# A decoder trunk on one core: the FFN's first product made token-stationary, its result turned by VectorE and moved by GpSimd's transfers

## The reference, cut to what matters

```
x = layer_norm(ALPHA * x + mixer(x) @ w_o)
up, gate = split(x @ w_in, 2)            # x 256 x 1024, w_in 1024 x 5632: up and gate 256 x 2816 each
up = causal_conv_over_tokens(up, width 3, one filter for each feature) + conv_b
f  = (gelu(up) * gate) @ w_out           # w_out 2816 x 1024
x = layer_norm(ALPHA * x + f)
```

## Time and profile before

| | |
|---|---|
| median of three runs | 600.32 us (600.27 to 600.74) |
| span of the profiled execution, first to last instruction | 598.3 us |
| TensorE matmuls busy | 589.4 us, 99%, 3216 instructions |
| VectorE busy | 464.9 us, 78% |
| ScalarE busy | 323.7 us, 54% |
| GpSimd busy | 50.5 us, 8% |
| read from HBM | 108.23 MB, 183 GB/s over the span |

### The profile page before, as it was taken

How to read it: one execution, slowest core, us unless ns; L and a number is a source line. 1 busy time by engine, 2 the same in 40 slices (tenths; PEclk the granted TensorE clock), 3 DMA queues, 4 the chain that set the end, 5 groups by cost and what they waited for, 6 DMA issues and landing times.

```text
span 598.3 us, 8585 instructions
## 1 busy us (share of the span) xinstructions
PE 589.4 (99%) x3216; PEld 501.1 (84%) x3216; DVE 464.9 (78%) x841; ACT 323.7 (54%) x520; POOL 50.5 (8%) x84
## 2 busy tenths in 40 slices
PE   8999999999999999999999999999999999999995
PEld 6887777898888888889888888889888888888894
DVE  4989994877777778777979797688677777777776
ACT  5756684265445444456445678935554555545430
POOL 6300000300000000000120003132000000000003
PEclk9999999999999999999999999999999999999998
DMA  8996865363556686554457955343755555755601
GB/s 306 296 341 215 261 186 189 139 223 109 184 191 209 211 280 211 192 169 173 172 203 222 302 177 186 108 140 101 251 191 182 188 170 204 242 172 201 210 2 70
DMA packets 82293, 116.38 MB, mean 195 GB/s; under 512 B 11292, under 2 KB 60236, under 8 KB 82252
## 3 DMA queue, kind: packets, MB, share of 16 engines
q1 hardware_dynamic: 80812, 111.64, 56.3%
q0 software_dynamic: 1152, 4.19, 2.1%
q10 hardware_dynamic: 288, 0.00, 0.0%
HBM read 108.23 MB, written 1.05 MB: 183 GB/s over the span
## 4 chain that ended last, share of the span: by engine, by line
PE 98%; DVE 1%; ACT 0%; DVEq 0%; issue 0%
PE wide L1294 18%; PE wide L1295 18%; PE wide L1296 18%; PE score L1501 11%; PE score L1507 6%; PE turn L1501 5%; PE outb L1501 5%; PE outb L1507 3%; PE turn L1507 3%; PE score L1307 1%; PE turn L1393 1%; PE outb L1419 1%; PE score L1296 1%; PE score L1295 1%; PE score L1294 1%; PE wide L1315 1%
## 5 line engine op out<-in xcount | busy, mean ns | idle before, releaser
L965 DVE TENSOR_TENSOR w_lo<-raw,w_hi 128x2048 fp32r<-128x2048 f32 (+1 forms) x120 | 211.0, 1776 | 60.6 <-ACT w_hi L772 60.4
L772 ACT ACTIVATE w_hi<-raw 128x2048 fp32r<-128x2048 f32 (+1 forms) x126 | 182.2, 1483 | 34.5 <-PE wide L1296 23.6
L1294 PE MATMUL wide<-w_hi,xT 128*128 128x512 f32 (+1 forms) x256 | 95.7, 374 | 0.3 <-DVE w_lo L1031 0.2
L1294 PE MATMUL wide<-w_hi,oT_hi 128*128 128x512 f32 x240 | 95.3, 397 | 0.0
L1295 PE MATMUL wide<-w_lo,oT_hi 128*128 128x512 f32 x240 | 93.7, 391 | 0.0
L1296 PE MATMUL wide<-w_hi,oT_lo 128*128 128x512 f32 x240 | 93.6, 390 | 0.0
L1296 PE MATMUL wide<-w_hi,xT 128*128 128x512 f32 (+1 forms) x256 | 93.0, 363 | 0.0
L1295 PE MATMUL wide<-w_lo,xT 128*128 128x512 f32 (+1 forms) x256 | 92.9, 363 | 0.0
L893 ACT ACTIVATE qT<-kT,conv_cols 128x256 f32<-128x256 f32 x36 | 21.7, 602 | 93.1 <-DVE kT L1198 93.1
L1501 PE MATMUL score<-xT,w_hi 128*128 128x512 f32 x288 | 68.3, 389 | 0.0
L1501 PEld LDWEIGHTS score<-xT,w_hi 128*128 128x128 f32 x288 | 53.9, 188 | 11.1
(11 more groups left out here) (182 smaller groups left out, 809.6 us busy)
## 6 DMA issues: line engine op xcount, KB each, us to landing
raw<-in_ffn_w_in SPq DMA_DIRECT2D x44, 1024.0 KB, 5.1
raw<-in_ffn_w_out SPq DMA_DIRECT2D x22, 1024.0 KB, 4.9
raw<-in_a_w_qkv SPq DMA_DIRECT2D x9, 1024.0 KB, 6.1
raw<-in_w_kv_shared SPq DMA_DIRECT2D x8, 1024.0 KB, 5.6
raw<-in_a_w_o SPq DMA_DIRECT2D x4, 1024.0 KB, 6.5
raw<-in_b_w_q SPq DMA_DIRECT2D x4, 1024.0 KB, 5.1
raw<-in_b_w_o SPq DMA_DIRECT2D x4, 1024.0 KB, 5.1
raw<-in_a_w_qkv SPq DMA_DIRECT2D x4, 512.0 KB, 7.7
```

The costliest lines, as they stand in the source:

```text
L772: ins = nc.scalar.activation(w_hi[c % RING][:, part], raw[c % RAW_RING][:, part], ACT.Copy)
L965: ins = nc.vector.tensor_tensor(w_lo[c % RING][:, part], raw[c % RAW_RING][:, part], w_hi[c % RING][:, part].bitcast(F32), ALU.subtract)
L1294: nc.tensor.matmul(dst, a_hi, b_hi, start=start, stop=False, skip_group_check=True)
```

## The change

- The first product of all groups is token-stationary. A chunk now holds four k-tiles of up and gate columns side by side (4 x 512 columns), loaded by two DMAs of 512 KB; a group is two such chunks. For each half of the tokens 8 products of 512 columns go to one bank: two banks a group, 48 matmuls. `features`, `last_features`, the first group's transposes on TensorE and VectorE's sums go.
- VectorE turns each bank in 32 x 32 blocks into `turned` (`turn_in`, two a group); GpSimd issues four DMAs of 32 partitions each (`in_move`) that make it feature-major in `in_moved`.
- ScalarE copies the up tiles out once more (`up`) beside the tap, and the gate is read from `in_moved`.
- The second product of a group comes behind the first product of the group two later; hidden tiles have a ring of 4 instead of 1 and 2. Behind the last first product stand now the whole second product of group 8, and then the quarters of groups 9 and 10 as before.
- The orders of ScalarE and VectorE are written anew, with the splits of a group's chunks ahead of its taps. Chunk numbers follow TensorE's new order. GpSimd loads the norm rows behind the sixth move.

```diff
+    def second_behind(i):
+        return [i - 2] if i >= 2 else []
@@ SP
+                def load_in(i):
+                    for h in range(2):
+                        load(ffn_chunk(layer, i, h),
+                             *[(lambda r, w=w: r.rearrange("p (k w n) -> p k w n", k=4, w=2)[:, :, w, :],
+                                w_in[:, 4 * h:4 * h + 4, w * DFF + i * 2 * P:w * DFF + (i + 1) * 2 * P]) for w in range(2)])
@@ GpSimd
+            def in_move(layer, i):
+                t = GROUPS * layer + i
+                pool.wait_ge(in_turned, ST * t + ST)
+                for a in range(4):
+                    pool.dma_start(in_moved[:, a, :], turned[32 * a:32 * a + 32, t % 2, :, :]).then_inc(in_carried, 16)
...
-                    pool.wait_ge(hidden_done, 2 * GROUPS * (n // 2) + GROUPS)
-                    load_norm(n)
+                    for i in range(GROUPS):
+                        in_move(n // 2, i)
+                        if i == GROUPS // 2:
+                            load_norm(n)
@@ ScalarE
+                def taps(i):
+                    t = GROUPS * layer + i
+                    act.wait_ge(in_carried, 64 * (t + 1))
                     for tt in range(2):
+                        if t > 0:
+                            act.wait_ge(conv_done, 2 * t + tt - 1)
+                        nc.scalar.activation(by_quarters(up[:, tt, :]), carried(tt), ACT.Copy)
+                        nc.scalar.activation(by_quarters(conv[:, tt, :]), carried(tt), ACT.Identity, ...).then_inc(tap_done, 1)
...
+                for i in range(GROUPS):
+                    split_hi(ffn_chunk(layer, i, 0) + RING)
+                    if i:
+                        make_h_hi(i - 1)
+                    if i < GROUPS - 1:
+                        split_hi(ffn_chunk(layer, i, 1) + RING)
+                        for n in second_behind(i):
+                            split_hi(ffn_chunk(layer, n, 2) + RING)
+                        taps(i)
+                        make_gelu(i)
+                    else:
+                        split_hi(ffn_chunk(layer, i, 1) + RING, 0)
+                        split_hi(ffn_chunk(layer, i, 1) + RING, 1)
+                        taps(i)
+                        make_gelu(i)
+                        make_h_hi(i)
+                        split_hi(ffn_chunk(layer, i - 2, 2) + RING, 0)
+                        split_hi(ffn_chunk(layer, i - 2, 2) + RING, 1)
@@ VectorE
+                def turn_in(i, st):
+                    t = GROUPS * layer + i
+                    dve.wait_ge(*((in_rows_done, t + 1) if st == 0 else (chunk_used, ffn_chunk(layer, i, 1) + 1)))
+                    if st == 0 and t >= 2:
+                        dve.wait_ge(in_carried, 64 * (t - 1))
+                    bank = (wide[0:2] if i == 0 else in_banks[(i - 1) % 2])[st]
+                    into = turned[:, t % 2, :, :].rearrange("p b (j s t) -> p b j s t", j=4, s=ST)
+                    nc.vector.transpose(into[:, :, :, st, :], bank[:, :].rearrange("p (j f b) -> p b j f", j=4, b=4)
+                                        ).then_inc(in_turned, 1)
...
+                for i in range(GROUPS):
+                    turn_in(i, 0)
+                    split_lo(ffn_chunk(layer, i, 0) + RING)
+                    turn_in(i, 1)
+                    if i:
+                        for tt in range(2):
+                            make_h_lo(i - 1, tt)
+                    if i < GROUPS - 1:
+                        split_lo(ffn_chunk(layer, i, 1) + RING)
+                        for n in second_behind(i):
+                            split_lo(ffn_chunk(layer, n, 2) + RING)
+                        add_taps(i)
+                        for tt in range(2):
+                            make_hidden(i, tt)
+                    else:
+                        split_lo(ffn_chunk(layer, i, 1) + RING, 0)
+                        split_lo(ffn_chunk(layer, i, 1) + RING, 1)
+                        add_taps(i)
+                        for tt in range(2):
+                            make_hidden(i, tt)
+                            make_h_lo(i, tt)
+                        if ffn_chunk(layer, i - 2, 2) + RING == SHARED:
+                            split_shared_lo()
@@ TensorE
+                def in_product(i):
+                    t = GROUPS * layer + i
+                    chunks = [ffn_chunk(layer, i, h) for h in range(2)]
+                    banks = wide[0:2] if i == 0 else in_banks[(i - 1) % 2]
+                    if i >= 3:
+                        pe.wait_ge(in_turned, ST * (t - 2) + ST)
+                    for h, st in ((0, 0), (1, 0), (0, 1), (1, 1)) if i == 0 else ((0, 0), (0, 1), (1, 0), (1, 1)):
+                        c = chunks[h]
+                        for k in range(4):
+                            kt = 4 * h + k
...
+                            if i == 0 and st == 0 and kt in (6, 7):
+                                x_transposes(2 * layer + 1, (kt - 4,))
...
+                            last = product(banks[st][:, :], xT_hi[:, kt, rs], xT_lo[:, kt, rs],
+                                           w_hi[c % RING][:, cols], w_lo[c % RING][:, cols], kt == 0, kt == KT - 1)
...
+                for i in range(GROUPS):
+                    in_product(i)
+                    for n in second_behind(i):
                         for st in range(ST):
                             for half in range(2):
+                                last = out_product(n, st, half)
                         last.then_inc(chunk_used, 1)
```

More of the change, by code:

```diff
@@ L349, in ffn_chunk, with raw_count @@
         if which == 2:
[L350 to L362, removed]
+            return base + (3 * i + 6 if i < GROUPS - 2 else 2 * GROUPS + i)
+        return base + (2 * i if i < 3 else 3 * i - 2) + which
+    def second_behind(i):
+        return [i - 2] if i >= 2 else []
+    IN_CHUNKS = {ffn_chunk(layer, i, h) for layer in range(LAYERS) for i in range(GROUPS) for h in range(2)}
+    def raw_count(c):
+        return sum(32 if n in IN_CHUNKS else 16 for n in range(c % RAW_RING, c + 1, RAW_RING))
     moves_ahead = {}
@@ L915, in ffn_group, with make_h_hi @@
-                    if peeled == "last":
-                        split_hi(cg + RING, 0)
-                        split_hi(cg + RING, 1)
-                    if peeled in ("second", "middle"):
-                        split_hi(cg + 1 + RING)
-                ffn_group(0, "first")
-                ffn_group(1, "second")
-                for i in range(2, GROUPS - 1):
-                    ffn_group(i, "middle")
-                ffn_group(GROUPS - 1, "last")
+                def make_h_hi(i):
+                    for tt in range(2):
+                        act.wait_ge(hidden_done, 2 * (GROUPS * layer + i) + tt + 1)
+                        if tt == 0 and i >= HIDDEN:
+                            act.wait_ge(chunk_used, ffn_chunk(layer, i - HIDDEN, 2) + 1)
+                        nc.scalar.activation(hT_hi[i % HIDDEN][:, tt, :], hidden[:, tt, :], ACT.Copy).then_inc(hhi_done, 1)
@@ L1529, in last_features @@
-                def last_features(banks, slot, free, free0, done0):
-                    for tt in range(2):
-                        pe.wait_ge(free, free0 + tt)
-                        for kt in range(KT):
-                            last = product(by_two(banks[tt])[:, 0, :], w_hi[slot][:, tile_cols(kt, tt)],
-                                           w_lo[slot][:, tile_cols(kt, tt)], xT_hi[:, kt, :], xT_lo[:, kt, :],
-                                           kt == 0, kt == KT - 1)
-                        last.then_inc(done0 if tt == 0 else chunk_used, 1)
@@ L1604, in _ @@
                         x_transposes(2 * layer + 2, (0,))
-                    last = second_product(ffn_chunk(layer, i, 2) % RING, int(final), st, half, stop=final)
+                    last = out_product(i, st, half)
                     if (st, half) == (1, 1):
```

288 lines of the change are left out of this document (67 added, 221 removed).

## The result

The changed kernel takes **616.9 us** (median of 4 runs, 614.9 to 619.4) where the kernel before takes 600.3: a ratio of 1.028, 95% interval 1.026 to 1.030. I had forecast 602.6, range 598.6 to 608.0: the sign was right, the size was not, and the time lies outside the range. The profiled execution has a span of 614.2 us, 15.9 over the one before, and 13.6 over the 600.6 of my sum.

The account below looks back on a forecast made before the run. TensorE, busy 99%, was taken to bound the kernel. Span 598.3 - 6.0 (products) + 7.6 (end idles) + 0.4 (restarts) + 0.3 (shared split) = 600.6; 2.0 more for timed runs gives 602.6 us, range 598.6 to 608.0.

Parts of the forecast that it names:

- TensorE's gain: FFN first products in the 512-column form: 3.0 us a layer saved, 6.0 in both; 0.14 per middle group.
- the LN wait: Group 0 of a layer's FFN: TensorE waits about 0.45 us for VectorE's layer-norm result before the first x transpose.
- D: Each group's move, from GpSimd's first issue to the last landing: taken as 5.6 us, between 4.4 and 8.0.
- Chunk 8: Stage start: this chunk's split ends near 156.4, TensorE wants it at 158.3; 1.9 us cover, no stall expected.
- Cost 0 up to D = 6.5: Stage start, two moves ahead of the chunk-8 split: no cost to TensorE while a move takes at most 6.5 us.
- rival 3: FFN groups: with moves of 8.0 us or more the loop binds and stays late; 613 us, chance 0.08.
- The end of a stage: Last group: TensorE idles 3.8 us a layer, 7.6 in both, awaiting its hidden tiles, ready at T + 12.0.
- The chain from landing to last lo: Stage end: copy, tap, conv tiles, hidden tiles and splits one after another on ScalarE and VectorE, 5.4 us in all.
- T: Stage end: the time when TensorE's spacing of the last first product, in_product(10), ends; later steps are counted from it.
- The loop: Middle groups: move, taps, conv, hidden, transposes and splits take about D + 8.2 = 13.8 us, under TensorE's 16.4.
- The clock: Rival, TensorE's stage-end gaps: a clock fall costs 2.5 us; 605.1 for one in two ends, 607.6 for both; chance 0.25.
- my 0.7 for restarts and the shared split: Stage ends: 0.4 us for TensorE's two restarts and 0.3 for VectorE's later shared split in layer 0.

Follow-up runs that it names:

- experiment 2: The changed kernel with its moves issued by SP instead of GpSimd, each ahead of a later chunk's load: 602.2 us, 1.003 of the kernel before.
- experiments 2 and 3: The second named: the changed kernel, GpSimd's moves kept, FFN weight loads cut to a quarter (w_in) and an eighth (w_out) of their bytes: 609.4 us, 1.016 of before.
- the first of experiment 4: The changed kernel with TensorE's end gaps filled by 24 (layer 0) and 11 (layer 1) matmuls whose result is overwritten: 613.1 us, 1.020 of before.
- experiment 5: The changed kernel with each layer's last group feature-stationary as before, read straight from PSUM without a move: 602.4 us, 1.004 of before.
- experiment 4's second pair: The version with SP's moves, with and without 11 and 10 filler matmuls in TensorE's end gaps: 599.3 us with, 602.2 without.

## Why the prediction was wrong

**TensorE's gain: right in kind, too low.** I had 3.45 a layer before the LN wait, measured 3.9. The forecast charged 0.03 for each change of section in the new groups; there is none. 48 matmuls take 10.88 and 24 take 5.44 (204.96 less 199.52), so the group is 16.32, 0.23 under the 16.55 of the earlier trace rows and not 0.14. As the extras went with the 256-column form, I put them down to it. The LN wait came as forecast, 0.50 for 0.45.

**D, the term that was mis-sized.** I took 5.6, with a landing of 3.1 to 3.9. Measured: landing 4.7, D mostly 6.4 to 7.2, and 8.4 and 8.0 for the first moves of the layers. The rows that I took it from the earlier trace rows mix two cases, and the trace of before could have shown it. Its four moves of this tile had D of 4.7 and 4.9 in windows with a DMA share of 0.87 and 0.56, and 5.5 and 8.0 in windows with a share of 1.00. The longest and one of the short ones (windows of the kernel before, from first issue to last landing; the last two columns are DMA share and GB/s):

```profile
328.59:336.58 7.99, 7.99 (x37) 6.61 (x36) 4.61 (x11) 4.47 (x6) 0.00 (x0) 1.00 1.00 342
351.99:356.92 4.93, 4.93 (x23) 4.05 (x23) 4.86 (x16) 3.51 (x8) 0.00 (x0) 1.00 0.56 120
```

I had read a DMA share of 0.40 for a middle group and of 0.93 at the first move and used the 0.40. But the share in the average stretch is not the share in the move's own: the moves of the kernel after fly in shares of 0.84 and more, but for the last two of layer 1 (0.73 and 0.46). VectorE's turn comes just behind a split, which frees a `raw` buffer, so the move sets out together with a load, 0.9 us behind it in 21 of 22 moves (experiment 2). Moves that met few loads or none landed sooner than my 3.1 to 3.9: after 2.8 us in the medians of experiments 2 and 3, and after 2.5 to 2.9 in layer 1's last move.

**Chunk 8: the cover was right, the cost wasn't.** "Cost 0 up to D = 6.5" held: SP's 5.2 and 5.5 give no gap, GpSimd's 8.4 and 6.9 give 2.3. It holds in size too. Two moves lie ahead of this split, so the cover is 13.0 for both together, and in all six gaps of the three kernels with GpSimd's moves and the splits behind the taps (the change, the first of experiment 4, and experiment 5) the gap is the sum of the two D less 13.0: 15.30 gives 2.33, 15.07 gives 2.10, 15.32 gives 2.35, 14.58 gives 1.62, 16.01 gives 3.02, 13.73 gives 0.75. I had seen this cliff and stood on its safe side with a D that was too small. The share of 0.93 that I named for rival 3 stood at just this place: the step that failed was to price the first moves by the average stretch.

**The end of a stage: structure right, two terms off.** The chain from landing to last lo is 5.3 for the forecast 5.4. With a punctual turn the idle is D less 1.8 (4.69 gives 2.91 in layer 0 of experiment 2), which at my D of 5.6 is the 3.8 of the sum. Layer 1, with D = 4.5 and a turn 0.6 behind T, idles 3.35: that this is near 3.8 is luck, a D too long against a turn too late. Layer 0 has D 6.4 for 5.6 and the turn at T + 2.1 for T + 0.2: ready at T + 14.9, not T + 12.0. The second term is one that I had argued away. The loop, D + 8.2 by my count and 14.9 at D = 6.5 measured, is under 16.3 and pays the late start back at some 1.4 us a group; 1.2 was left at group 9, whose move of 8.8 us then made its loop longer than a group.

**The clock: a rival, and it happened, twice.** I gave it 0.25, at 2.5 a fall, which is 5 us at 0.50; no run shows that length, the falls in mid-kernel lasted 3.41 and 6.83. The two cost 2.0 and 1.7 by the windows; in experiment 4's second pair the fillers gave back 1.4 a gap by the medians, 1.6 by the traces. In these runs the gaps of 2.10, 2.33 and 2.35 us left the clock at 1.0; those of 2.75, 2.91 (two), 2.98, 3.02 and 3.35 were followed by 3.41 us at 0.50; those of 4.66, 4.94 and 6.69 by 6.83 us, part of it still idle. At the end of the kernel before, TensorE had been idle for 3.0 us (since its last matmul) when the granted clock went to 0.50, and my forecast gap of 3.8 was longer. By these rows the fall was the likelier case, and the main forecast should have carried it.

**The drain: missing.** 4.0 us of the 13.6. "GpSimd issues four DMAs of 128 KB a group; it is idle there" put the issuing at nothing: I had costed what GpSimd's DMAs do while they run and not what they leave. The trace of before holds a drain of 1.77 for 8 DMAs, from which alone the growth couldn't be had.

So over the sum: end idles +2.4, clock +3.7, chunk 8 +4.4, drain +4.0, TensorE -0.8 (7.8 less 1.0 for 6.0): 13.7, where 13.6 is to be explained; my 0.7 for restarts and the shared split and the 0.4 ahead of the first FFN are too small to be told apart. Of the rivals, the third (the loop binds from D = 8 on: late splits, idles of 6 and more) was the nearest at 613, and I gave it 0.08. Its stalls came without its condition: no loop of D = 8 was needed, a long move at the start and one near the end were enough.

## What to carry to other kernels

Price a small transfer by the DMA share in the stretch where it will fly, just behind the event that also frees a load buffer, and ask whether its issuer lets the loads run past it: the same 128 KB landed after 2.8 us from the loads' own queue and after 4.7 from another. A gain per group is worth little if one group at a stage's end must make the whole round trip with nothing to cover it; keep the old form for that group (602.4 against 616.9). And an idle of TensorE of 3 us cost about half as much again in clock here (1.6 to 1.7 us); if it can't be removed, try to fill it.

## What the hardware showed that I had not expected

- GpSimd's drain at the program's end was longer with more DMAs issued by GpSimd: 1.77 us for 8, 8.31 for 88, 8.96 for 96, that is 0.082 us for each move of 128 KB. In the kernel before it ended 3.2 us ahead of SP's and cost nothing; in the kernel after it outlasted SP's by 4.0 us, all of it in the span.
- A DMA of 128 KB landed alike from GpSimd and from SP where few loads were in flight: 2.8 us in the median of both (experiments 3 and 2). I had put SP's spread down to its queue.
- Each low clock in mid-kernel lasted 3.41 or 6.83 us in these traces, the second behind gaps of 4.66 us and more; and 21 matmuls of no use made the kernel 2.8 us faster than two gaps of 2.9 and 2.7 us did.
- Not settled: how much of experiment 4's first saving was the quicker move of its group 9; why single moves take 8 us and more with a load beside them where most take 6.5; and what in a DMA of GpSimd's its drain grows by, their number or their bytes and pieces.
